# Weaving the second layer's mixer, in two token halves, into the expert retrieval of a two-layer decoder on one Trainium2 core

## The chip, the cores and the metric

The program runs on one core of one Trainium2 chip. All data are float32. The metric is the device time of one execution in microseconds (us). The time before is the median of three executions.

## The reference

Two decoder layers work on 512 tokens of width 1024. Each layer adds a mixer and then a channel mixer (PEER, a retrieval of experts) to the residual stream x; a last RMSNorm follows.

```
x = x + even_mixer(rmsnorm(x))          # layer 0: gated MLP and sparse attention
x = x + peer_0(rmsnorm(x))
x = x + odd_mixer(rmsnorm(x))           # layer 1: gated linear recurrence, 8 heads
x = x + peer_1(rmsnorm(x))
out = rmsnorm(x)

# peer: per token, 8 heads, the best 16 of 128 x 128 experts
s = (x @ w_q) . sub_keys                # two scores of 128 keys for each head
experts, gate = top16(sums of the two top16), softmax
u = u_tab[experts]; v = v_tab[experts]  # rows of 1024 + 1024 numbers
x += sum(gate * gelu(x . u) * v)

# odd_mixer, for each head: q, f, i, g = h @ w_in
fg = lb + (1 - lb) * sigmoid(f);  k = 1 - fg
state = diag(fg) state + k i^T;   o = q . state      # along the tokens, causal
out = (rmsnorm(o) * silu(g)) @ w_out
```

The recurrence of a token needs only tokens before it. The retrieval of a token needs only that token.

## The kernel before, in words

Every engine's program is written out by hand in full, in order, and the engines meet only by semaphores. There are four stages, one after the other: the even mixer, the retrieval of layer 0, the odd mixer, the retrieval of layer 1.

**Retrieval.** The 512 tokens are four blocks of 128. A block has 8 heads with 16 experts each, so there are 128 slots in a block and 512 in a layer. In a slot one expert row of 8 KB (u and v) is fetched for each of the 128 tokens, 1.05 MB, by an indirect DMA that POOL issues (L471) into one of 8 buffers of `gath` (region_g). VectorE forms the dot product of u and the normed token (L954, out in place). ScalarE's `weigh` takes the gelu (L619), multiplies by the gate (L620) and writes a diagonal matrix (L622). TensorE's `pair` multiplies this by v in two matmuls of 512 columns and adds up a whole block in PSUM banks 0 and 1 (L1338). POOL issues the gather of slot s + 8 once TensorE has done slot s. Between the dot products VectorE does the ranking (top 16, lookups) of the next head, and TensorE its query matmuls (L1293) and scores (L1308); the scores are copied from PSUM by VectorE (L876). ScalarE's softmax exponential (L613) needs another activation table than gelu, which is loaded again after it (the ACT_TABLE_LOAD rows).

**Odd mixer.** It starts when the last block of layer 0 has been added to x, with `normed_transposed(1)`. Per head, TensorE projects all 512 tokens (`projections`, L1388, L1391), builds the causal 128 x 128 products at 7 levels of a binary tree of distances and a diagonal (L1428), transposes and forms the state terms (L1435 to L1458). VectorE computes the running sum (L1054), the distances (L1067, L1068), the decayed queries (L1090) and puts each level into `attn` under a mask (L1072). ScalarE takes sigmoid (L678), logarithm (L688) and exponentials (L691), three activation tables. POOL multiplies the keys (L505). The weights come in slabs of 2 MB, one per head, into region_g, where the gather buffers also lie. Then the output projection, and the retrieval of layer 1 begins with its first routing and with the gathers after the last output projection.

Every engine waits for `primed` at the start; SyncE sets it after it has raised each event's semaphore by its starting value, so that waits for negative counts pass.

## Time and profile before

| | |
|---|---|
| median of three executions | 3622.25 us (3618.0 to 3626.44) |
| the profiled execution | 3623.28 us, span 3621.6 us |
| TensorE busy | 3090.3 us, 85% |
| VectorE busy | 2328.7 us, 64% |
| ScalarE busy | 1363.4 us, 38% |
| POOL busy | 1179.0 us, 33% |
| gathers (software queue) | 1073.81 MB, 71.5% of 16 engines' span |
| other transfers | 63.63 MB, 4.5% |
| mean granted TensorE clock | 0.939 |

Busy time is the sum of an engine's instructions; a group's mean is that of one instruction, and a float32 matmul is two of them (two MATMUL and two LDWEIGHTS records). What an instruction waited for stands behind it as the releaser of the idle time. The span has four stretches, which the windows of the trace show by their DMA share: up to 525 us, the first retrieval up to 1823 us, the odd mixer up to 2308 us, and the second retrieval.

### The profile page before, as it was taken

The page shows a single profiled execution, that of the slowest core. Times are in us where ns is not written, and L with a number is a line of the kernel's source. Part 1 is how long each engine was busy: PE and PEld are TensorE (multiplying, and loading weights), DVE is VectorE, ACT ScalarE, POOL GpSimd, SP SyncE. Part 2 cuts the span into 40 slices and gives each one's busy share as a digit, 9 for nine tenths or more (in the row PEclk, how much of TensorE's full clock was granted, in tenths as well). Part 3 has the DMA queues.
Part 4 walks back from the last instruction along what each step waited for, and adds up shares of the span by engine and source line. Part 5 has one row for each costly group of instructions (what it writes and reads, how often), then busy time and mean ns, then how long its engine had stood idle before and what let it go on. Part 6 is the DMA issues. An engine that isn't in the chain of part 4 may idle for free.

```text
span 3621.6 us, 31355 instructions
## 1 busy us (share of the span) xinstructions
PE 3090.3 (85%) x8800; PEld 1559.5 (43%) x8800; DVE 2328.7 (64%) x5547; ACT 1363.4 (38%) x3865; POOL 1179.0 (33%) x1164
## 2 busy tenths in 40 slices
PE   6988889888888888888878887888888888888887
PEld 3656644333333333333346665433333333333333
DVE  1144437777777777777745554577777777777777
ACT  0022204444444444444412222244444444444443
POOL 2000014444444434444401111243444444334443
PEclk9865589999999999999989998999999999999999
DMA  4120019999999999999941101499999999999998
GB/s 159 59 105 1 0 76 421 421 421 413 421 421 421 397 421 421 401 422 421 421 203 47 47 24 59 204 421 421 421 407 421 421 400 422 421 421 401 421 422 336
DMA packets 155535, 1139.45 MB, mean 315 GB/s; under 512 B 17888, under 2 KB 18144, under 8 KB 22240
## 3 DMA queue, kind: packets, MB, share of 16 engines
q0 software_dynamic: 147456, 1073.81, 71.5%
q1 hardware_dynamic: 7904, 63.63, 4.5%
q8 instruction: 70, 1.15, 0.1%
q14 instruction: 105, 0.86, 0.1%
HBM read 1134.23 MB, written 2.10 MB: 314 GB/s over the span
## 4 chain that ended last, share of the span: by engine, by line
DMA 42%; PE 38%; DVE 8%; ACT 6%; issue 3%; POOL 2%; DVEq 0%; SPq 0%; POOLq 0%; ACTq 0%
DMA region_g<-in_uv_dram,experts 42%; PE ps L1338 13%; DVE region_g L954 4%; PE ps L1388 4%; PE ps L1273 3%; PE ps L1391 2%; PE ps L1259 2%; PE ps L1293 2%; PE ps L1162 2%; PE ps L1221 2%; PE ps L1149 2%; PE ps L1428 1%; POOL region_g L471 1%; ACT region_c L622 1%; PE ps L1249 1%
## 5 line engine op out<-in xcount | busy, mean ns | idle before, releaser
L1338 PE MATMUL ps<-region_g,region_c 128*128 128x512 f32 x4096 | 1982.8, 613 | 370.2 <-ACT region_c L622 322.3
L954 DVE CUSTOM_DVE_ANT_0 region_g<-region_g,region_h 128x1024 f32<-128x1024 f32 x1024 | 1254.9, 1226 | 621.6 <-DMA region_g<-in_uv_dram,experts 607.2
L471 POOL DMA_INDIRECT region_g<-in_uv_dram,experts x1024 | 1089.4, 1064 | 1561.5 <-PE ps L1338 1413.5
L1338 PEld LDWEIGHTS ps<-region_g,region_c 128*128 128x128 f32 x4096 | 728.5, 191 | 1395.2 <-ACT region_c L622 767.5
L619 ACT ACTIVATE region_c<-region_c 128x1 f32<-128x1 f32 x1024 | 207.0, 202 | 1284.7 <-DVE region_c L954 1281.3
L622 ACT ACTIVATE region_c<-ident_z,region_c 128x128 f32<-128x128 f32 x1024 | 411.0, 401 | 33.5
L620 ACT ACTIVATE region_c<-region_c,gate 128x1 f32<-128x1 f32 x1024 | 301.4, 294 | 33.3
L1293 PE MATMUL ps<-region_a,region_h 128*128 128x256 f32 x1088 | 277.3, 379 | 0.0
L1293 PEld LDWEIGHTS ps<-region_a,region_h 128*128 128x128 f32 x1088 | 206.7, 190 | 139.0 <-issue 124.4
L1388 PE MATMUL ps<-region_h,region_g 128*128 128x512 f32 x256 | 134.6, 668 | 23.2 <-DVEq L1052 21.9
L1391 PE MATMUL ps<-region_g,region_h 128*128 128x256 f32 x512 | 118.8, 379 | 0.0
L1273 PE MATMUL ps<-region_g 128*128 128x512 f32 x256 | 114.6, 608 | 1.6 <-ACT region_g L603 0.8
L409 POOL TENSOR_SCALAR rstd<-stat 128x1 f32<-128x1 f32 (+2 forms) x9 | 3.6, 406 | 334.7 <-DVEq L848 306.7
L505 POOL TENSOR_TENSOR region_c<-region_g,region_c 128x256 f32<-128x256 f32 x56 | 42.5, 758 | 201.2 <-ACT region_c L691 131.6
L409 POOL TENSOR_SCALAR rstd<-mean 128x4 f32<-128x4 f32 x12 | 4.5, 377 | 306.3 <-DVEq L1115 156.3
L1391 PEld LDWEIGHTS ps<-region_g,region_h 128*128 128x128 f32 x512 | 94.1, 190 | 14.5 <-issue 3.8
L619 ACT ACT_TABLE_LOAD x66 | 84.7, 1283 | 14.6 <-DVE region_c L954 13.4
L1259 PEld LDWEIGHTS ps<-region_c 128*128 128x128 f32 x320 | 70.6, 328 | 38.0 <-issue 25.8
L1072 DVE COPY_PREDICATED region_c<-level_mask,ps 128x512 f32<-128x512 int32 x64 | 46.9, 733 | 59.1 <-PE ps L1428 58.7
L1388 PEld LDWEIGHTS ps<-region_h,region_g 128*128 128x128 f32 x256 | 51.9, 217 | 76.3 <-issue 74.6
L1259 PE MATMUL ps<-region_c 128*128 128x64 f32 x320 | 76.6, 426 | 8.9 <-ACT region_c L598 8.9
L954 DVE DVE_READ_ACCUMULATOR2_ANT region_c<- 128x1 f32 x1024 | 84.1, 82 | 0.0
(211 smaller groups left out, 2475.1 us busy)
## 6 DMA issues: line engine op xcount, KB each, us to landing
region_g<-in_uv_dram,experts POOLq DMA_INDIRECT x1024
region_g<-in_w_odd_dram SPq DMA_DIRECT2D x8, 2048.0 KB, 8.0
region_a<-in_w_even_dram SPq DMA_DIRECT2D x1, 5216.0 KB, 20.4
region_a<-in_w_even_dram SPq DMA_DIRECT2D x1, 4096.0 KB, 15.5
region_g<-in_w_out_e_dram SPq DMA_DIRECT2D x1, 4096.0 KB, 13.8
region_g<-in_w_out_o_dram SPq DMA_DIRECT2D x1, 4096.0 KB, 12.4
x_res<-in_x_dram SPq DMA_DIRECT2D x4, 512.0 KB, 5.0
region_a<-in_keys_dram SPq DMA_DIRECT2D x2, 1024.0 KB, 29.3
```

The lines of the kernel that those rows point to most:

```text
L471: g.indirect_dma_start(out=gath[:, k % NBUF, :], out_offset=None, in_=tab, in_offset=bass.IndirectOffsetOnAxis(ap=experts[:, e * TOPK + k: ...
L619: link(a.activation(gact[:, q:q + 1], dots[:, q:q + 1], ACT.Gelu_apprx_tanh))
L620: link(a.activation(wts[:, q:q + 1], gact[:, q:q + 1], ACT.Copy, scale=gate[:, e, k:k + 1]))
L622: a.activation(diag[:, k % NBUF, :], ident, ACT.Copy, scale=wts[:, q:q + 1]).then_inc(diag_ready.sem, 1)
L954: v.tensor_tensor_reduce(out=gath[:, buf, 0:D_MODEL], in0=gath[:, buf, 0:D_MODEL], in1=XNb[b % 2], scale=1.0, scalar=0.0, op0=ALU.mult, op ...
L1149: i = t.matmul(PS[:, 6 + ch % 2, :], We[:, c, TM_ALL + ch * P:TM_ALL + (ch + 1) * P], hT[:, c, :], start=c == 0, stop=c == KC - 1)
L1259: t.matmul(PS[:, 6 + par, br * HD:(br + 1) * HD], pTs[:, par, br * SEQ + kt * P:br * SEQ + (kt + 1) * P], vsw[:, kt, br, e * HD:(e + 1) * ...
L1273: i = t.matmul(PS[:, OUT_BANKS[tb] + j, :], mixT[:, c, tb * P:(tb + 1) * P], w[:, c, j * 512:(j + 1) * 512], start=c == 0, stop=c == KC - 1)
L1293: i = t.matmul(PS[:, 4, 0:256], hTb[:, c, :], wq[:, c, ds(hcol * 256, 256)], start=c == 0, stop=c == KC - 1)
L1338: i = t.matmul(PS[:, j, :], diag[:, k % NBUF, :], gath[:, k % NBUF, D_MODEL + j * 512:D_MODEL + (j + 1) * 512], start=first and e == 0 and ...
L1388: last = t.matmul(PS[:, j, :], W[:, c, j * P:(j + 1) * P], hT[:, c, :], start=c == 0, stop=c == KC - 1)
L1391: last = t.matmul(PS[:, 2 + tb // 2, (tb % 2) * 256:(tb % 2 + 1) * 256], hT[:, c, tb * P:(tb + 1) * P], W[:, c, 256:512], start=c == 0, st ...
```

## The change

- The order of the work is now one loop over 1024 slots, `for s in range(SLOTS)`, on each of VectorE, ScalarE, TensorE and POOL. The retrievals of both layers follow each other without a break. All other work of the second layer is cut into pieces, each with a slot number; a generator yields them, and `run(pieces, s)` emits those that are due after slot s.
- Layer 1's mixer works on halves of 256 tokens (two blocks). Half 0 is computed in slots 256 to 511, beside the retrieval of layer 0's blocks 2 and 3, half 1 in slots 512 to 767, beside layer 1's blocks 0 and 1. The state of each head is carried over in `carry`. Heads start 20 slots into such a stretch and every 19 slots.
- Routing (queries and scores) is done for two blocks at once, in four jobs, with transposed queries straight from the matmul; ScalarE copies the scores into a ring, VectorE no longer does.
- The weights come as 1 MB slabs into three buffers in region_a: 1 for each routing head, 2 for each recurrent head, 4 for the output projection. Each half and each pair of blocks fetches its weights again.
- In the two mixed stretches, slots 5 and 13 of each 16 are not multiplied by TensorE: VectorE adds gate * v to x (`row_added`, two slots later).
- Some of the recurrence's work moves from VectorE to ScalarE (the forget gate's affine step, the key decay, squares); all seven levels get their exponential in one instruction of 1792 columns.
- The starting values of the semaphores and `primed` are gone; waits for negative counts are left out of the program.

```diff
+HALF = 2 * P
+BLOCK = P_HEADS * TOPK
+PHASE = 2 * BLOCK
+SLOTS = DEPTH * TB * BLOCK
+HEADS_AT, HEAD_PACE = 20, 19
+DVE_ROWS = ((), (5, 13), (5, 13), ())
...
-            for e in events:
-                sp.sem_inc(e.sem, e.prime)
-            sp.sem_inc(primed, 1)
...
+            for q in range(2):
+                for h in range(C_HEADS):
+                    for part in range(2):
+                        slab(head_slab(q, h, part), w_odd[h][:, part * 2048:(part + 1) * 2048])
+                for j in range(4):
+                    slab(out_slab(q, j), w_out_o[:, 2 * j:2 * j + 2, :].rearrange("p c n -> p (c n)"))
+                for h in range(P_HEADS):
+                    routing_slab(2 + q, h)
...
+            def slab(i, dram):
+
+                if i >= 3:
+                    after(sp, *slab_user[i - 3])
+                sp.dma_start(slabs[i % 3][:, 0:KC * 256], dram).then_inc(slab_in[i % 3], 16)
...
+                    yield t0 + 1
+                    act.wait_ge(qf_done.sem, qf_done.at(n))
+                    act.wait_ge(ig_done.sem, ig_done.at(n))
...
+                    a.activation(kk, fgr, ACT.Identity, scale=-1.0, bias=ones[:]).then_inc(sig_ready.sem, 1)
+                    yield t0 + 2
+                    act.wait_ge(fg_ready.sem, fg_ready.at(n))
+                    a.activation(bb, fgr, ACT.Ln).then_inc(lf_ready.sem, 1)
...
+                    yield t0 + 6
+                    act.wait_ge(dd_ready.sem, dd_ready.at(n))
+                    a.activation(D, D, ACT.Exp)
+                    a.activation(eb, bb, ACT.Exp)
+                    for t in range(2):
+                        i = a.activation(kd[:, t * P:(t + 1) * P], bb[:, t * P:(t + 1) * P], ACT.Exp, scale=-1.0,
+                                         bias=bb[:, (t + 1) * P - 1:(t + 1) * P])
+                    i.then_inc(e_ready.sem, 1)
...
+                    yield t0 + 3
+                    dve.wait_ge(lf_ready.sem, lf_ready.at(n))
+                    link(v.tensor_tensor_scan(bb, scan_keep, bb, 0.0, ALU.mult, ALU.add))
...
+                    yield t0 + 7
+                    dve.wait_ge(e_ready.sem, e_ready.at(n))
...
+            def row_added(s):
+
+                n, k = s // TOPK, s % TOPK
+                c, xb = (n % 2) * TOPK + k, X[:, n // P_HEADS % TB, :]
+                dve.wait_ge(w_ready.sem, w_ready.at(dve_n(s)))
+                after(dve, vd_done, dve_n(s) - 1)
+                v.scalar_tensor_tensor(xb, gath[:, s % NBUF, D_MODEL:ROW], wts[:, c:c + 1], xb, ALU.mult, ALU.add
+                                       ).then_inc(vd_done.sem, 1)
...
+            for s in range(SLOTS):
+                n, k = s // TOPK, s % TOPK
+                dot_product(s)
+                if s >= 2 and on_dve(s - 2):
+                    row_added(s - 2)
+                if s % BLOCK == 2 and s > BLOCK:
+                    block_out(s // BLOCK - 1)
+                if k < 7:
+                    late_ranking(n + 1, k)
+                if k >= 12:
+                    early_ranking(n + 2, k - 12)
+                run(pieces, s)
...
+                        if h + 1 < C_HEADS and d < 19:
+                            projections(q, h + 1, d - 3)
...
+            for s in range(SLOTS):
+                if not on_dve(s):
+                    row_product(s)
+                run(pieces, s)
```

TensorE, in the middle of a head of the odd mixer, before: L1391 is a projection, L1428 a level, L1435 the key transposes, L1441 the state terms.

```order
L1428 MATMUL ps<-region_c 128x128 x4
L1391 MATMUL ps<-region_g,region_h 128x256 x4
L1428 MATMUL ps<-region_g 128x128 x4
L1391 MATMUL ps<-region_g,region_h 128x256 x4
L1435 MATMUL ps<-ident_z,region_c 128x128 x4
L1391 MATMUL ps<-region_g,region_h 128x256 x5
L1441 MATMUL ps<-region_g,region_c 128x128 x4
```

The same place in the change: L1566 is the row product of a slot, L1434 and L1437 are projections of the next head, L1475 two levels of a half, L1512 the key transposes.

```order
L1566 MATMUL ps<-region_g,x_res 128x512 x2
L1434 MATMUL ps<-region_a 128x256 x2
L1475 MATMUL ps<-region_a 128x128 x4
L1566 MATMUL ps<-region_g,x_res 128x512 x2
L1434 MATMUL ps<-region_a 128x256 x2
L1475 MATMUL ps<-region_a 128x128 x4
L1512 MATMUL ps<-ident_z,region_a 128x128 x2
L1437 MATMUL ps<-region_a 128x256 x2
L1566 MATMUL ps<-region_g,x_res 128x512 x2
```

Where projections and levels followed each other, a row product now stands before each group; one slot (between L1512 and the next L1437) has none, since VectorE takes its row.

ScalarE, at the start of a head in the change, after the last squares of the head before: L773, L774 and L780 are a slot's gelu, gate and diagonal, L724 to L729 the sigmoids, copies and the affine steps, L732 the logarithm.

```order
L724 ACT_TABLE_LOAD
L724 ACTIVATE region_a<-ps 128x256
L725 ACTIVATE region_a<-ps 128x256
L726 ACTIVATE region_a<-ps 128x256
L727 ACTIVATE region_a<-ps 128x256
L728 ACTIVATE region_a<-region_a,lb 128x256
L729 ACTIVATE region_a<-region_a,ones 128x256
L773 ACT_TABLE_LOAD
L773 ACTIVATE region_a<-region_a 128x1
L774 ACTIVATE region_a<-region_a,gate 128x1
L732 ACT_TABLE_LOAD
L732 ACTIVATE region_a<-region_a 128x256
```

Before, a sigmoid, a logarithm and the exponentials each loaded their table once in a head; now the gelu of the next slot needs its own table after each of them.

VectorE, at the same place in the change: L1153 is a slot's dot product with its accumulator, L989 to L993 the three operations that wait for the sigmoids, L996 the running sum that waits for the logarithm, L954 and L955 the distances.

```order
L989 TENSOR_SCALAR region_a<-region_a 128x256
L991 TENSOR_TENSOR region_a<-ps,region_a 128x256
L993 TENSOR_TENSOR region_a<-ps,region_a 128x256
L1153 ISA region_g,region_a<-region_g,region_h 128x1024
L1153 ISA region_a 128x1
L996 SCALAR_TENSOR_TENSOR region_a<-alibi,region_a 128x256
L1153 ISA region_g,region_a<-region_g,region_h 128x1024
L1153 ISA region_a 128x1
L954 TENSOR_TENSOR region_a<-region_a 128x128
L955 TENSOR_TENSOR region_a<-region_a 128x128
```

Between two operations that wait for ScalarE stands one dot product (and at most places a step of the ranking).

## Rows read from the trace of the kernel before

**Rows 1.** Windows: us, busy of each engine (xcount), granted clock, DMA share, GB/s.
```profile
525.00:1823.00 1298.00, 1110.26 (x2801) 495.34 (x2801) 955.41 (x2332) 577.72 (x1736) 545.56 (x514) 0.99 1.00 414
1823.00:2308.00 485.00, 408.47 (x1720) 278.34 (x1719) 238.57 (x450) 114.51 (x170) 54.13 (x77) 0.91 0.17 67
2308.00:3606.00 1298.00, 1110.16 (x2798) 494.46 (x2797) 958.24 (x2333) 577.69 (x1736) 548.71 (x516) 0.99 1.00 414
```
**Rows 2.** Timeline, POOL, the first gather of each retrieval and the last of the first: start, us.
```profile
525.31 1.23 POOL L471 DMA_INDIRECT region_g<-in_uv_dram,experts  x1 [44.29 <-PE ps L1273]
...
1807.10 0.94 POOL L471 DMA_INDIRECT region_g<-in_uv_dram,experts  x1 [0.31 <-issue]
...
2307.90 1.05 POOL L471 DMA_INDIRECT region_g<-in_uv_dram,experts  x1 [44.26 <-PE ps L1273]
```
**Rows 3.** Timeline, VectorE, the last dot product of the first retrieval and the first of the second.
```profile
1823.14 1.23 DVE L954 CUSTOM_DVE_ANT_0 region_g<-region_g,region_h 128x1024 f32<-128x1024 f32 x1 [1.21 <-DMA region_g<-in_uv_dram,experts]
...
2317.82 1.22 DVE L954 CUSTOM_DVE_ANT_0 region_g<-region_g,region_h 128x1024 f32<-128x1024 f32 x1 [0.18 <-DVE region_c L890]
```
**Rows 4.** Groups, 700 to 1700 us, shapes apart: group xcount | busy, mean ns | idle before, releasers.
```profile
L1338 PE MATMUL ps<-region_g,region_c 128*128 128x512 f32 x1585 | 766.4, 612 | 140.2 <-ACT region_c L622 116.9 <-DVEq L1000 17.1 <-issue 3.1
L954 DVE CUSTOM_DVE_ANT_0 region_g<-region_g,region_h 128x1024 f32<-128x1024 f32 x396 | 485.4, 1226 | 243.9 <-DMA region_g<-in_uv_dram,experts 239.1 <-DVE gstat L902 0.9 <-DVE gate L923 0.7
...
L622 ACT ACTIVATE region_c<-ident_z,region_c 128x128 f32<-128x128 f32 x396 | 158.9, 401 | 13.0
L620 ACT ACTIVATE region_c<-region_c,gate 128x1 f32<-128x1 f32 x396 | 116.6, 294 | 12.9
...
L619 ACT ACTIVATE region_c<-region_c 128x1 f32<-128x1 f32 x397 | 80.3, 202 | 501.3 <-DVE region_c L954 499.9
...
L619 ACT ACT_TABLE_LOAD x25 | 32.1, 1283 | 0.4
...
L876 DVE COPY region_c<-ps 128x256 f32<-128x256 f32 x25 | 10.5, 419 | 0.0
...
L627 ACT ACTIVATE region_c<-ps 128x256 f32<-128x256 f32 x25 | 9.2, 367 | 11.0 <-PE ps L1293 11.0
...
L860 DVE SCALAR_TENSOR_TENSOR region_h<-x_res,rstd,region_h 128x1024 f32<-128x1024 f32 x3 | 3.8, 1279 | 0.0
```
**Rows 5.** Timeline, TensorE: one row product alone and three in sequence.
```profile
1798.70 1.98 PE L1338 MATMUL ps<-region_g,region_c 128*128 128x512 f32 x4 [0.95 <-ACT region_c L622]
...
1801.38 5.31 PE L1338 MATMUL ps<-region_g,region_c 128*128 128x512 f32 x12
```
**Rows 6.** Groups, 1860 to 2260 us, the second layer's mixer, shapes apart.
```profile
L1391 PE MATMUL ps<-region_g,region_h 128*128 128x256 f32 x512 | 118.8, 379 | 0.0
...
L1428 PE MATMUL ps<-region_c 128*128 128x128 f32 x448 | 62.6, 286 | 12.3 <-DVE region_c L1090 11.8 <-issue 0.4
...
L1072 DVE COPY_PREDICATED region_c<-level_mask,ps 128x512 f32<-128x512 int32 x64 | 46.9, 733 | 59.1 <-PE ps L1428 58.7
...
L505 POOL TENSOR_TENSOR region_c<-region_g,region_c 128x256 f32<-128x256 f32 x56 | 42.5, 758 | 201.2 <-ACT region_c L691 131.6 <-PE ps L1428 69.6
L691 ACT ACTIVATE region_c<-region_c 128x512 f32<-128x512 f32 x56 | 35.3, 630 | 111.0 <-DVE region_c L1068 111.0
L1068 DVE TENSOR_TENSOR region_c<-region_g 128x256 f32<-128x256 f32 x56 | 28.1, 501 | 1.9
L1067 DVE TENSOR_TENSOR region_c<-region_g 128x256 f32<-128x256 f32 x56 | 24.2, 433 | 8.7 <-POOL region_c L505 6.4 <-DVE region_c L1072 0.9
...
L1054 DVE TENSOR_TENSOR_SCAN region_g<-alibi,region_g 128x512 f32<-128x512 f32 x8 | 9.8, 1224 | 1.6 <-ACT region_g L688 0.5
...
L1051 DVE TENSOR_TENSOR region_g<-ps,region_c 128x512 f32<-128x512 f32 x8 | 5.5, 692 | 1.2
```
**Rows 7.** Timeline, VectorE's first instruction.
```profile
6.61 0.06 DVE L718 MEMSET slope<- 128x1 f32 x1 [6.61 <-SPq L340]
```
**Rows 8.** The page's DMA issues: xcount, KB each, median us to landing.
```profile
region_g<-in_w_odd_dram SPq DMA_DIRECT2D x8, 2048.0 KB, 8.0
```

More of the change, by code:

```diff
@@ new lines, in dve_n, with row_freed, run, started @@
+        def dve_n(s):
+            return dve_rows[s + 1] - 1
+        def row_freed(eng, s):
+            if s < 0:
+                return
+            if on_dve(s):
+                after(eng, vd_done, dve_n(s))
+            else:
+                after(eng, slot_done, pe_n(s))
+        def run(pieces, tick):
+            while pieces[1] is not None and pieces[1] <= tick:
+                pieces[1] = next(pieces[0], None)
+        def started(gen):
+            return [gen, next(gen, None)]
@@ new lines, in final_norm @@
+                                       ).then_inc(fin_done.sem, 1)
+            link.reset()
+            pieces = started(mixer_pieces())
+            residual(0)
+            residual(1)
+            run(pieces, -90)
+            residual(2)
+            for step in range(4):
+                early_ranking(0, step)
+            for step in range(7):
+                late_ranking(0, step)
+            residual(3)
+            for step in range(4):
+                early_ranking(1, step)
+            run(pieces, -1)
@@ new lines, in mixer_pieces, with row_product @@
+            def mixer_pieces():
+                yield from routing_pieces(0)
+                yield from routing_pieces(1)
+                for q in range(2):
+                    yield from recurrence_pieces(q)
+                    yield from routing_pieces(2 + q)
+            def row_product(s):
+                b = s // BLOCK
+                first = all(on_dve(r) for r in range(b * BLOCK, s))
+                last = all(on_dve(r) for r in range(s + 1, (b + 1) * BLOCK))
+                if first:
+                    if b:
+                        after(pe, acc_out, b - 1)
+                    else:
+                        pe.wait_ge(wo_out.sem, wo_out.at(3))
+                pe.wait_ge(diag_ready.sem, diag_ready.at(pe_n(s)))
+                for j in range(2):
+                    i = t.matmul(PS[:, j, :], diag[:, pe_n(s) % NBUF, :],
+                                 gath[:, s % NBUF, D_MODEL + j * 512:D_MODEL + (j + 1) * 512], start=first, stop=last)
+                i.then_inc(slot_done.sem, 1)
```

1380 lines of the change are left out of this document (702 added, 678 removed).

## The prediction

> **What bounds the kernel now.** I read the windows first [rows 1]. Of the span, two stretches of 1298 us are retrieval, with the DMA engines busy all the time at 414 GB/s, and between them lie 485 us, the odd mixer, with a DMA share of 0.17. The timeline gives the edges [rows 2, 3]: the last dot product of layer 0 starts at 1823.14 us, the first gather of layer 1 at 2307.90 us. So for **484.8 us no gather moves**, although the gathers decide everything else. In a retrieval the groups say the same [rows 4]: VectorE's idle time before its dot products ends with a gather's landing (239.1 of 243.9 us), so a slot costs 1298 / 512 = 2.535 us, which is the DMA's time. The engines beside it have room: per slot VectorE is busy 955.4 / 512 = 1.866 us, TensorE 2.17 us, ScalarE 1.13 us, POOL 1.07 us [rows 1]. The change wants to put the mixer into that room.
>
> How deep is the buffer? The last gather was issued at 1807.10 and used at 1823.14 us [rows 2, 3], so 16.0 us, some 6 of the 8 slots, lie in the DMA queues. A stall of an engine of less than some 10 us costs nothing, as long as its mean load is under the DMA's. What counts is the mean over a head, 19 slots.
>
> **The sum**, against the profiled execution (3623.28 us, its span 3621.6 us; the median of the runs, 3622.25 us, is 1 us less).
>
> 1. The gap goes: **-484.8 us**. The restart goes too: the second retrieval's first dot product comes at 2317.82, 9.9 us after its first gather [rows 2, 3], against 2.5 us in the stream: **-7.4 us**.
>
> 2. Weights that now pass in the gather stream. In MB: a routing head's slab is 1.05 of queries and 0.13 of keys, 1.18. Job 0 leaves five of its eight to the stream (5.9), job 1 eight (9.4), jobs 2 and 3 sixteen (18.9), the two output projections 8.4: 42.6 MB outside the heads. Where the DMA binds, each MB costs 1 / 0.414 = 2.42 us: **+103 us**. There the other engines keep up: a routing head takes TensorE 16 matmuls of 256 columns at 0.464 us (below) and four of 128, some 8.5 us, with 6.1 row products of 1.77 us (below) 19.3 us in 7 slots, against (7 x 1.05 + 1.18) / 0.414 = 20.6 us of DMA. The heads' own slabs, 16 x 2.1 MB, are in the next term.
>
> 3. A recurrent head, 19 slots. **DMA:** (19 x 1.05 + 2.1) / 0.414 = 53.2 us.
>  **TensorE:** row products, 14 of 16, are 16.6. Three in sequence took 5.31 us, 1.77 us each, one alone 1.98 us [rows 5]; the group's mean is 766.4 / 396 = 1.94 us [rows 4]. I take 1.77, as a loaded TensorE has no waits between them: 29.4 us. 32 projection matmuls of 256 columns at 118.8 / 256 = 0.464 us: 14.8 us. 16 level matmuls of 128 columns at 62.6 / 224 = 0.28 us and ten other small ones at the same price: 7.3 us [rows 6]. Sum 51.5 us, with 1.94 us 54.3 us. It is under the DMA or equal to it.
>  **VectorE:** 19 x 1.866 = 35.5 us, less the score copy (0.42 us in each 16 slots, [rows 4]) 35.0 us. Its own small gaps: 2.535 - 1.866 - 239.1 / 396 = 0.065 us for a slot, 1.2 us. The rows it adds, 19 x 2 / 16 = 2.4, at the price of the 1024-column operation with two tensor inputs, 1.28 us [rows 4]: 3.0 us. The recurrence [rows 6]: an operation of 512 columns takes 0.692 us, one of 256 0.433 us, so one of 128 some 0.30 us. 14 distances and 7 decayed queries at 0.30 are 6.3 us; four products of 256 columns 1.7; eight masked copies, 0.733 us at 512 columns and so 0.45 at 256, 3.6; the running sum, 1.22 us at 512, 0.7; the floor of the gate 0.3; the state two of 128, 0.6; two outputs of 128, 0.6. Together 13.8 us. That is **53.0 us** of work, just what the DMA needs.
>  **The waits inside it.** VectorE waits for ScalarE three times in a head, and each time only one dot product and a step of ranking (1.8 us) lie between. A gelu, gate and diagonal take 0.20 + 0.29 + 0.40 us and a table load 1.28 us [rows 4]; activations of 256 and 512 columns take 0.37 and 0.63 us [rows 4, 6], so one of 1792 some 1.95 us. Sigmoids: 1.28 + six activations 2.3 = 3.6 us against 1.8: 1.8 us of wait. Logarithm: 1.28 for gelu, 0.9, 1.28, 0.4 = 3.9 us against 3.0 (one dot product and three operations): 0.9 us. Exponentials: 1.28 + 1.95 + 0.4 + 0.5 = 4.1 us against 1.8: 2.3 us. Sum 5.0 us. In about one head of five a softmax with its two table loads falls into one of these: 0.5 us. No row shows this interplay, so I bound it: nothing if the DMA is late anyway, 10 us if each wait doubles.
>  **POOL against VectorE:** seven key products in each head, while VectorE works. The two halves of a distance are alike in size, and take 0.501 and 0.433 us on average [rows 6]; put down to POOL altogether, as an upper reading of this row, that is 0.07 us for each product, 0.5 us a head.
>  So VectorE needs 53.0 + 5.0 + 0.5 + 0.5 = **59.0 us** for 19 slots that took 19 x 2.535 = 48.2 us. **+10.8 us for each of 16 heads, +173 us.** With the DMA alone it would be +5.1, with full contention and doubled waits +18.
>
> 4. Edges: before the first head of a half TensorE has 16 projection parts in 8 slots, 3.4 us a slot against 2.5, and ScalarE waits for the last; the output projection's parts weigh 1.7 us a slot. I take 4 us for each half, **+8 us** (0 to 20).
>
> 5. The start. All engines waited until 6.61 us for SyncE's semaphores [rows 7]: -6.1 us. Ahead of the first gather TensorE now routes two blocks instead of one, with a second set of transposes and its copy, +5 us. Together **-1 us**.
>
> 3623.3 - 484.8 - 7.4 + 103 + 173 + 8 - 1 = **3414 us**.
>
> The tail (last slot to stored rows) keeps its steps. POOL has 20.2 us of gathers in a head and adds 7 products of some 0.4 us: covered, since it is idle until TensorE frees a slot. ScalarE has 21.4 us of slots and some 16 us of its own (six table loads, 7.7, and activations) in 59: covered on average.
>
> **Two rules of the Trainium skill.** Behind the 0.07 us: the page SBUF — State Buffer, section Who interferes with whom, has VectorE and GpSimd lock each other out for a whole instruction when VectorE reads two SBUF tensors and GpSimd reads SBUF. By it each key product (0.758 us at 256 columns, an estimated 0.43 at 128) would hold VectorE up for its full length, 3.0 us a head instead of 0.5, and the sum would be 3454 us; the row of the distances shows much less. Behind the routing slabs, whose rows are 1 KB long: the page DMA: Bandwidth & Descriptors, section Why small descriptors are slow, gives three extra cycles for each packet, 35 for 32 at 1 KB; no run here shows it, and the sum would be an estimated 8 us more.
>
> **Rivals.**
> - **The DMA binds throughout.** If ScalarE runs ahead of my count, all 76.2 MB of slabs cost 184 us and the mixer nothing more: 3623.3 - 484.8 - 7.4 - 1 + 184 = 3314 us. For it: the 16 us queue. Against it: VectorE's 53.0 us leave no room for any wait.
> - **The engines wait for each other.** TensorE's six middle slots of a head carry levels as well: 6 x 1.77 + 6 x 0.93 + 5.5 = 21.7 us, against 18.6 us at 3.1 us a slot. VectorE waits for these levels two slots later, and then TensorE for VectorE's rows. With 64 us a head it is 80 us more, 3494 us. For it: 54.3 us of TensorE at the price of single rows. Against it: the two slots of distance are 6 us.
> - **Slower: the slabs come late.** The second slab of a head is asked for when the head before has been projected, and TensorE wants it 6 slots (18.6 us) later. The gathers of [rows 2, 3] took 16.0 us through the full queue; a slab that has to queue behind gathers and another slab would stall TensorE in the middle of its rows. TensorE's 51.5 us plus the stall pass 59 us from 7.5 us on. To lose the whole gain, a head would need 59.0 + 209 / 16 = 72.1 us, so a stall of 21 us, a slab landing after 39 us. At 45 us it is 78.5 us a head, 312 us more: 3726 us. For it: nothing in this trace shows both queues loaded. Against it: 2 MB with no gathers beside them took 8.0 us [rows 8], and at half the rate 16.
> - **The stream breaks.** If the routing of layer 1's first blocks is not ready at slot 512, gathers stop after all. It ends only 8 slots before. The price would be some 60 us of the 485 saved, inside my range.
>
> **Chances.** My case 60%. DMA throughout 15%. Mutual waits 20%. Slabs late enough to be slower 4%, about no change 1%. The range of 8 in 10 reaches from 3325 (between my case and the first rival) to 3530 (the second rival with doubled waits). A measurement of this kernel tells 0.2%, 7 us. Faster by more: 0.95, within: 0.01, slower: 0.04.
>
> **What would show it.** Right: no stretch without gathers between 525 us and the end; windows inside the heads at some 373 GB/s (22.0 MB in 59 us), with VectorE busy over 0.9 and its waits on ScalarE's sigmoid, logarithm and exponential (1.8, 0.9, 2.3 us); outside them 414 GB/s. Wrong: heads at 414 GB/s (first rival), TensorE busy all the time or VectorE waiting for L1475 (second), TensorE waiting for a landing from in_w_odd (third).

## The result and the profile after

The changed kernel takes 3436.09 us (median, 3431.08 to 3439.38) against 3622.61 us for the kernel before in the same series: ratio 0.9484, 95% interval 0.9466 to 0.9503. Forecast were 3414 us, range 3325 to 3530. The profiled execution took 3432.9 us, its span is 3430.4 us.

The windows of the changed kernel; they answer to [rows 1]: the first stretch of retrieval without heads, the heads of half 0, the routing behind them, the heads of half 1, and the last stretch. Columns: us, busy of PE, PEld, DVE, ACT, POOL, granted clock, DMA share, GB/s.

```profile
543.00:1232.00 689.00, 588.73 (x1596) 285.63 (x1596) 447.36 (x1141) 297.25 (x867) 275.10 (x259) 0.99 1.02 415
1283.00:1755.00 472.00, 408.75 (x1390) 240.64 (x1389) 381.34 (x995) 268.09 (x652) 212.72 (x222) 0.95 0.95 374
1793.00:2004.00 211.00, 184.50 (x589) 106.05 (x590) 137.06 (x330) 85.38 (x246) 84.80 (x77) 0.98 1.02 413
2055.00:2530.00 475.00, 413.94 (x1398) 244.77 (x1398) 378.30 (x987) 267.52 (x652) 215.11 (x222) 0.94 0.94 371
2770.00:3417.00 647.00, 512.59 (x1022) 183.43 (x1022) 438.30 (x1084) 278.08 (x831) 267.61 (x257) 0.97 1.00 414
```

The stretch at 67 GB/s is gone. There are two kinds of stretch now: 414 GB/s outside the heads, some 372 inside. The timeline of POOL with the first gather, which answers to [rows 2], and that of VectorE with the first and the last dot product, to [rows 3]:

```profile
531.40 1.25 POOL L568 DMA_INDIRECT region_g<-in_uv_dram,experts  x1 [29.30 <-PE ps L1362]
```

```profile
543.60 1.23 DVE L1153 CUSTOM_DVE_ANT_0 region_g<-region_g,region_h 128x1024 f32<-128x1024 f32 x1 [0.18 <-DVE region_c L1081]
...
3416.70 1.23 DVE L1153 CUSTOM_DVE_ANT_0 region_g<-region_g,region_h 128x1024 f32<-128x1024 f32 x1 [1.22 <-DMA region_g<-in_uv_dram,experts]
```

Since every slot has one dot product, their starts cut the span exactly. Before, a slot of the stream was 2.5206 us from dot product to dot product. Now the 719 slots outside the heads take 1926.5 us, 114.1 more than at that price; the 304 slots of the heads take 471.5 + 475.1 = 946.6 us, 180.4 more; the first dot product comes 8.4 us later than before (535.2 us); the tail is 1.9 us shorter. With the 492.2 us of the gap: 3621.6 - 492.2 + 114.1 + 180.4 + 8.4 - 1.9 = 3430.4 us, the measured span.

What VectorE waits for in the heads of half 0 (1283 to 1755 us): us in total, times, longest.

```profile
DVE region_a L969 <- PE ps L1475: 23.1, 17, 4.6
DVE region_a L1040 <- POOL ost L521: 19.6, 6, 5.7
DVE region_a L961 <- ACT region_a L741: 13.9, 8, 3.0
DVE region_a L996 <- ACT region_a L732: 7.5, 8, 1.4
DVE region_a L989 <- ACT region_a L729: 7.4, 3, 6.1
```

And TensorE, in the same stretch:

```profile
PE ps L1566 <- ACT x_res L780: 58.5, 30, 6.3
```

Per head VectorE is busy 381.34 / 8 = 47.7 us and waits 11.3; TensorE is busy 408.75 / 8 = 51.1 us and waits 7.9, nearly all for a slot's diagonal (L780). Neither is busy throughout. The waits for the levels (L1475) and for POOL's root of the output (L521) are not in the forecast's account of a head.

TensorE's granted clock falls in the heads too, to 0.95 and 0.94 from 0.99 in the first stretch. In half 0, 44 of the 471.5 us lie at the lower of its two levels (1.2 GHz instead of 2.4), in nine short stretches; each begins during a wait of TensorE of 2.6 to 6.3 us or at most 1.1 us behind it. So TensorE pays for some of its waits a second time.

### The profile page after: what moved, and what is told of

Read it like the earlier page. It is cut to its first block, busy times and chain, and to the rows that moved or that the text cites. A ratio compares the mean times of both kernels' runs of the same rounds, so it can differ in the third digit from the quotient of the medians.

```text
span 3430.4 us, 30594 instructions
## 1 busy us (share of the span) xinstructions
PE 2927.8 (85%) x8568; PEld 1548.4 (45%) x8568; DVE 2226.7 (65%) x5636; ACT 1459.7 (43%) x3950; POOL 1258.2 (37%) x1254
## 4 chain that ended last, share of the span: by engine, by line
PE 43%; DMA 31%; DVE 12%; ACT 10%; issue 3%; POOL 2%; DVEq 0%; SPq 0%; POOLq 0%; ACTq 0%
DMA region_g<-in_uv_dram,experts 29%; PE ps L1566 19%; DVE region_g L1153 6%; PE ps L1400 3%; PE ps L1437 3%; PE ps L1348 2%; PE ps L1251 2%; PE ps L1310 2%; PE ps L1362 2%; PE ps L1238 2%; PE ps L1434 2%; DMA region_a<-in_keys_dram 1%; ACT x_res L780 1%; POOL region_g L568 1%; PE ps L1475 1%
## 5 line engine op out<-in xcount | busy, mean ns | idle before, releaser
L1566 PE MATMUL ps<-region_g,x_res 128*128 128x512 f32 x3840 | 1896.2, 624 | 414.6 <-ACT x_res L780 379.3
L1153 DVE CUSTOM_DVE_ANT_0 region_g<-region_g,region_h 128x1024 f32<-128x1024 f32 x1024 | 1255.4, 1229 | 572.6 <-DMA region_g<-in_uv_dram,experts 561.2
L1566 PEld LDWEIGHTS ps<-region_g,x_res 128*128 128x128 f32 x3840 | 705.1, 196 | 1350.3 <-ACT x_res L780 733.6
L773 ACT ACTIVATE region_a<-region_a 128x1 f32<-128x1 f32 x1024 | 208.7, 204 | 1372.9 <-DVE region_a L1153 1367.5
L780 ACT ACTIVATE x_res<-ident_z,region_a 128x128 f32<-128x128 f32 x960 | 387.4, 404 | 31.2
L774 ACT ACTIVATE region_a<-region_a,gate 128x1 f32<-128x1 f32 x1024 | 304.5, 297 | 33.4
L1400 PE MATMUL ps<-region_a 128*128 128x256 f32 x1024 | 243.8, 383 | 5.5 <-DMA region_a<-in_keys_dram 4.3
L1400 PEld LDWEIGHTS ps<-region_a 128*128 128x128 f32 x1024 | 196.5, 192 | 83.5 <-issue 55.4
L773 ACT ACT_TABLE_LOAD x110 | 141.1, 1283 | 6.4 <-DVE region_a L1153 4.4
L1434 PE MATMUL ps<-region_a 128*128 128x256 f32 x512 | 133.7, 391 | 0.0
L1437 PE MATMUL ps<-region_a 128*128 128x256 f32 x512 | 131.2, 383 | 0.0
L1434 PEld LDWEIGHTS ps<-region_a 128*128 128x128 f32 x512 | 101.4, 199 | 63.3 <-issue 54.7
L1437 PEld LDWEIGHTS ps<-region_a 128*128 128x128 f32 x512 | 97.7, 192 | 59.3 <-issue 51.8
L969 DVE COPY_PREDICATED region_a<-level_mask,ps 128x256 f32<-128x256 int32 x128 | 56.7, 443 | 61.7 <-PE ps L1475 52.5
L1153 DVE DVE_READ_ACCUMULATOR2_ANT region_a<- 128x1 f32 x1024 | 84.6, 83 | 0.0
L1162 DVE SCALAR_TENSOR_TENSOR x_res<-region_g,region_a,x_res 128x1024 f32<-128x1024 f32 x64 | 82.0, 1281 | 0.0
L765 ACT ACT_TABLE_LOAD x63 | 80.8, 1283 | 1.1
```

The lines of the kernel that those rows point to most:

```text
L765: a.activation(gexp, best, ACT.Exp, bias=gstat[:, 0:1], accum_out=gstat[:, 1:2]).then_inc(gexp_out.sem, 1)
L773: link(a.activation(gact[:, c:c + 1], dots[:, c:c + 1], ACT.Gelu_apprx_tanh))
L774: i = a.activation(wts[:, c:c + 1], gact[:, c:c + 1], ACT.Copy, scale=gate[:, n % 2, k:k + 1])
L780: a.activation(diag[:, pe_n(s) % NBUF, :], ident, ACT.Copy, scale=wts[:, c:c + 1]).then_inc(diag_ready.sem, 1)
L1153: v.tensor_tensor_reduce(out=u_, in0=u_, in1=XNr[n // P_HEADS % 3], scale=1.0, scalar=0.0, op0=ALU.mult, op1=ALU.add, accum_out=dots[:, c: ...
L1162: v.scalar_tensor_tensor(xb, gath[:, s % NBUF, D_MODEL:ROW], wts[:, c:c + 1], xb, ALU.mult, ALU.add).then_inc(vd_done.sem, 1)
```

## Experiments

Each kernel ran in one series with the kernel before; ratios are to it (its median lies between 3622.6 and 3625.2 us in the five series). "Less" and "slower" in us are against the 3436.09 us of the changed kernel. Runs 3, 4 and 11 are single executions. "Heads" are the 152 slots of half 0 and of half 1, by the dot products (160 in runs 10 and 12). A head's tick d is the d-th slot after its start; a piece of tick d stands behind that slot's work.

**1. POOL's root earlier.** The head's root is placed ahead of one more gather in POOL's program.

```diff
-                        yield head_tick(q, h) + 19
+                        yield head_tick(q, h) + 18
                         pool.wait_ge(oss_ready.sem, oss_ready.at(n))
```

> POOL does the small root for a head's output right after it has issued the gather of slot t0 + 26 instead of t0 + 27, so before it waits for slot t0 + 19 to come free. Theory (in the heads VectorE is the bound, and its waits add up): its wait for this root, 25.6 us in the eight heads of the first half (3.2 us a head), mostly goes; 2 to 3 us a head, 16 heads, less what shows up in another wait: the changed kernel's 3436 us become 3395 to 3415 us, the heads 56 to 57 us instead of 58.9 us. Rival 1 (the DMA engines bind in the heads): no change, heads 58.9 us. Rival 2 (TensorE and VectorE hold each other up at the levels): the wait moves to the levels, less than 10 us gained.

Measured: 3435.17 us, ratio 0.9474 (0.9459 to 0.9490): no difference to 0.9484 that can be told. VectorE's waits in the heads of half 0:

```profile
DVE region_a L969 <- PE ps L1475: 30.4, 18, 5.8
DVE region_a L989 <- ACT region_a L729: 15.4, 8, 6.2
...
DVE region_a L996 <- ACT region_a L732: 10.5, 8, 1.9
DVE region_a L1040 <- POOL ost L521: 10.5, 5, 3.6
```

The root's wait is half as long, and what it gave was taken by the next wait in program order, the sigmoids of the next head (7.4 before), and by the levels. The heads take 478.4 and 475.3 us; run 8, which changes nothing in them, also has 478.4 and 474.6, so some 7 us of half 0 are scatter. In run 8 it goes with TensorE's clock. Its window of half 0:

```profile
1281.00:1760.00 479.00, 416.58 (x1391) 244.65 (x1390) 382.32 (x995) 267.06 (x652) 210.63 (x222) 0.93 0.94 369
```

The same program of a head, with 65 instead of 44 us at the lower level, keeps TensorE busy 7.8 us more and takes 6.9 us more. VectorE's busy time is the same within 1 us. Not all of the scatter is the clock: run 7, also unchanged in the heads, has 474.3 us at 0.95.

**2. VectorE adds no rows.** `DVE_ROWS` is empty in all stretches.

> No row is added by VectorE; TensorE multiplies all 16 of 16 in the mixed stretches too. Theory (VectorE bounds the heads): it loses 2.4 x 1.28 = 3.0 us of work a head and POOL no longer waits for rows that VectorE frees late; TensorE gets 4.2 us more, 51.5 + 4.2 = 55.7 us, which is under 58.9 us. So the heads get 1 to 3 us shorter, and the whole 15 to 45 us faster than the changed kernel, if nothing else binds. Rival 2 (TensorE and VectorE hold each other up at the levels): TensorE at 55.7 us plus its wait is the bound, heads 60 us or more, the whole 15 us or more slower. Outside the heads, routing beside 16 of 16 rows: TensorE 7 x 1.77 + 8.5 = 20.9 us in 7 slots against 20.6 us of DMA, no change or a few us slower.

Measured: 3450.31 us, ratio 0.9515 (0.9499 to 0.9531), 14 us slower. The heads take 484.8 and 482.9 us. The window of the heads of half 0 and VectorE's largest waits in it:

```profile
1285.00:1770.00 485.00, 437.90 (x1470) 254.47 (x1469) 359.26 (x976) 274.16 (x671) 208.72 (x222) 0.96 0.95 365
```

```profile
DVE region_a L969 <- PE ps L1475: 37.6, 24, 4.6
DVE region_a L1040 <- POOL ost L521: 34.4, 6, 8.6
```

VectorE's busy time falls from 381.3 to 359.3 us, TensorE's rises from 408.8 to 437.9 us. So a head is not VectorE's work plus fixed waits: 2.8 us less of that work a head made it 1.7 and 1.0 us longer in the two halves, and VectorE's waits for the levels and for POOL's root, which stands behind slots that TensorE frees, grew. This is the side of the expectation's rival. The rows on VectorE are worth their place.

**3, 4. Fewer bytes.** In 3 each slab of a head after the first three brings an eighth of its bytes (`dram[:, 0:256]`), in 4 each routing slab of the queries after the first three does (`k_ = 1` of 8 chunks). The matmuls run on what lies in the buffers: seven eighths of those weights are left out.

> Left out: of each recurrent head's slab after the first three only 1 of 8 KB in each partition is loaded, so these projections use old weights and the output is another. 29 slabs shrink by 0.92 MB, 27 MB in all. Theory (VectorE and its waits bound the heads): the heads stay at 58 to 59 us, the whole is within 10 us of the changed kernel's profiled execution (3433 us). Rival 1 (the DMA binds in the heads): 27 x 2.42 = 65 us faster.

> Left out: of each routing head's query weights after the first three slabs only one of eight chunks is loaded, so the scores are others and other experts are fetched, as many as before. 29 slabs shrink by 0.92 MB, 26.6 MB in all. Theory (outside the heads the DMA binds, and every MB costs 2.42 us): 64 us faster than the changed kernel, about 3369 us; phase 0 takes 689 - 29 = 660 us. If rows of 1 KB cost more than their bytes, more than that: 70 to 90 us. Rival (TensorE binds while it routes beside the rows in the two mixed stretches): less than 45 us.

Measured: 3424.92 us and 3366.18 us. The window of the heads of half 0 in 3, and that of the first 256 slots in 4:

```profile
1283.00:1754.00 471.00, 408.01 (x1388) 240.59 (x1387) 381.18 (x995) 266.16 (x653) 212.14 (x222) 0.95 0.91 349
```

```profile
543.00:1202.00 659.00, 584.44 (x1594) 289.08 (x1595) 448.32 (x1148) 295.22 (x864) 289.60 (x258) 0.98 1.01 417
```

With 7% fewer GB/s the heads take the same 471 and 475 us: there the DMA does not bind. Outside, 4 moves its fewer bytes at 417 GB/s, as before (415), and 689 us become 659. By the dot products the stretches outside the heads take 69.4 us less, where the bytes alone say 64: there the DMA binds by bytes.

**5. Projections early.** The 16 projection parts of the next head stand two to a slot at the head's ticks 3 to 8, and at 15 to 18, instead of one to a slot from 3 to 18.

```diff
+PARTS_AT = {3: (0, 1), 4: (2, 3), 5: (4, 5), 6: (6, 7), 7: (8, 9), 8: (10, 11), 15: (12,), 16: (13,), 17: (14,), 18: (15,)}
...
-                        if h + 1 < C_HEADS and d < 19:
-                            projections(q, h + 1, d - 3)
+                        if h + 1 < C_HEADS:
+                            for part in PARTS_AT.get(d, ()):
+                                projections(q, h + 1, part)
```

> The projections of the next head move from the ticks 3 to 18 (one each) to the ticks 3 to 8 (two each) and 15 to 18. Theory (a head is a first part in which VectorE waits for ScalarE and TensorE waits with it, and a second part in which TensorE carries rows, projections and levels and VectorE waits for it): the wait of VectorE for the levels, 3.4 us a head, and part of the wait of TensorE for ScalarE, 58.5 us in eight heads, go away, a head falls from 59.0 to 54 to 55 us, the kernel by 60 to 70 us, to about 3370 us. Rival (VectorE's own work and its waits for ScalarE set a head alone): the wait only moves, as it did when POOL's root came earlier, and the time stays at 3436 +- 5 us. Second rival (the second slab of a head is asked for late): TensorE waits for the slab of in_w_odd at tick 4, and the time rises.

Measured: 3399.92 us, ratio 0.9384 (0.9369 to 0.9400), 36 us less. The heads take 455.5 and 455.6 us. VectorE's and TensorE's waits (half 0):

```profile
DVE region_a L1041 <- POOL ost L522: 16.6, 6, 3.9
DVE region_a L970 <- PE ps L1476: 15.2, 9, 4.2
```

```profile
PE ps L1568 <- ACT x_res L781: 45.3, 26, 6.8
```

The direction is the theory's, the size 55% of it. The same TensorE work in another order gives 16 and 19.5 us a half: the forecast's account of a head, which had TensorE hidden at 51.5 us, can't give that. It was not the first part of the head that gained. TensorE's waits before the slots of ticks 7 to 10 fall from 20.5 to 2.3 us in half 0; those at ticks 2 to 4 stay (35.7 and 36.6 us).

**6. Key products on VectorE.** The seven products of a head move from POOL to VectorE, behind the decayed queries of the same levels.

> The seven key products of a head move from POOL to VectorE. Theory (VectorE is held up while POOL reads SBUF for them): the decayed queries fall from a mean of 0.468 to 0.29 us, some 2.7 us of contention a head go, VectorE's added work is 7 x 0.20 = 1.4 us, so a head falls by 1.3 us and the kernel by 20 us, more if the levels come earlier too. Rival (the longer decayed queries are only waits for ScalarE's exponential in other dress, no contention): VectorE gets 1.4 to 3 us a head more and the kernel is 20 to 50 us slower.

Measured: 3423.82 us, ratio 0.9447 (0.9431 to 0.9463), 12 us less; heads 469.0 and 469.6 us. First what happens in the changed kernel, POOL and VectorE at the same time (start, us, ..., count):

```profile
1314.32 3.09 POOL L547 TENSOR_TENSOR region_a<-region_a 128x128 f32<-128x128 f32 x7
```

```profile
1311.44 0.90 DVE L961 TENSOR_TENSOR region_a<-region_a 128x128 f32<-128x128 f32 x4 [2.99 <-ACT region_a L741]
...
1314.44 3.32 DVE L961 TENSOR_TENSOR region_a<-region_a 128x128 f32<-128x128 f32 x3
```

Four products alone take 0.90 us, three under POOL's seven 3.32 us, and both engines end within 0.4 us of each other. The groups of the decayed queries in the changed kernel, then in this one (L954), with the key products (L960):

```profile
L961 DVE TENSOR_TENSOR region_a<-region_a 128x128 f32<-128x128 f32 x56 | 23.0, 468 | 14.0 <-ACT region_a L741 13.9
```

```profile
L954 DVE TENSOR_TENSOR region_a<-region_a 128x128 f32<-128x128 f32 x56 | 12.8, 286 | 13.9 <-ACT region_a L734 13.8
L960 DVE TENSOR_TENSOR region_a<-region_a 128x128 f32<-128x128 f32 x56 | 12.6, 281 | 0.0
```

The contention is real: (23.0 - 12.8) / 8 = 1.3 us a head here, with the two products behind it (0.526 and 0.524 us each, now 0.414) some 1.5. My 2.7 was one head's worst. The Trainium skill's rule (SBUF — State Buffer, Who interferes with whom: an operation of VectorE with two inputs in SBUF and one of GpSimd that reads SBUF exclude each other) agrees with the 3.32 us. VectorE's added work is 1.6 us, about as much, and its busy time falls by only 4.0 and 3.3 us a half. So the contention does not account for the 12 us; what else gives them is not shown, and the two halves' 2.5 and 5.5 us are within their scatter.

**7. Routing weights by head.** The host lays `w_q` out so that a slab is one row of 8 KB in each partition instead of eight of 1 KB.

```diff
-        "w_q": arr("peer_w_q").reshape(2, 8, 128, 2048).transpose(0, 2, 1, 3),
+        "w_q": arr("peer_w_q").reshape(2, 8, 128, 8, 256).transpose(0, 2, 3, 1, 4).reshape(2, 128, 8, 2048),
```

> The routing weights are laid out head by head, so that a slab is one row of 8 KB per partition instead of eight of 1 KB. Bytes and the rest stay. Where the DMA binds, outside the heads, 40 slabs of 1.05 MB pass in 1 KB packets. By bytes alone: no change. By the three extra cycles of the Trainium skill's page DMA: Bandwidth & Descriptors (35 for 32): 8 us less. By the packets' mean times (47 to 49 ns for these, 39 ns for those of linear slabs): up to 19 us less. All of it has to show in the stretches outside the heads, phase 0 and the routing after the heads; the heads stay at 471 and 475 us.

Measured: 3418.31 us, ratio 0.9432 (0.9417 to 0.9448), 18 us less than the changed kernel's. By the dot products the three stretches with routing slabs fall from 688.7, 248.8 and 240.3 to 682.7, 243.7 and 236.1 us, together 15.3 us; the heads stay within 3 us. The queue of the slabs on the two pages (packets, MB, share), the changed kernel's and this one's:

```profile
q1 hardware_dynamic: 50576, 102.96, 8.0%
```

```profile
q1 hardware_dynamic: 21904, 102.96, 7.5%
```

The same bytes in 28672 fewer packets. They belong to 32 slabs (the expectation says 40), of which three are loaded ahead of the stream, so 25984 packets go in these stretches: 15.3 us of 16 engines are 9.4 ns for each. The packets' own mean times agree: 48.8 ns for one of 1 KB, 315.9 for one of 8 KB, 39.5 for each KB. The Trainium skill's page DMA: Bandwidth & Descriptors, section Why small descriptors are slow (three extra cycles a packet, 35 for 32 at 1 KB), gave an estimated 8 us; the sign agrees, the size measured here is twice that. Run 4 took the same number of packets away with their bytes and gained only 5 us beyond the bytes; why not 15 is open.

**8. The start's order.** In job 0 ScalarE takes the second block's squares before it copies the first block's transposed rows.

> At the start ScalarE takes the squares of the second block before it copies the transposed rows of the first. Theory (TensorE is idle for 4.44 us before the transposes of the second block because of this order): the first gather comes 4 to 5 us earlier, at 527 us instead of 531.4, and the kernel is 4 to 5 us faster. Rival (the first gather waits for the slabs or for TensorE's queue): no change.

Measured: 3432.30 us (3427.24 to 3437.85), ratio 0.9469 (0.9453 to 0.9485), not to be told from 0.9484 by itself. In the trace the first gather starts at 527.10 us instead of 531.40 and the first dot product at 539.3 instead of 543.6: 4.3 us, as expected.

**9. Four together** (5, 6, 7, 8).

> The four edits together: projections early, key products on VectorE, routing weights by head, the start's order. If their gains add, 35.6 + 11.7 + 17.2 + 3.2 = 67.7 us below the changed kernel's 3436, 3368 us. The gains outside the heads (routing weights 17, start 3) have nothing in common with the others and must stay. In the heads the projections and the key products may gain less together (both free VectorE or what it waits for): 3368 to 3380. Or more, if TensorE, now with levels on time, lets VectorE use the contention's time in full: 3355 to 3368.

Measured: 3381.67 us, ratio 0.9327 (0.9312 to 0.9343). The gains don't add (54 of 68 us): the heads take 461.1 and 456.0 us, no less than with 5 alone, so the key products on VectorE are worth nothing that can be told once the levels come in time. Outside the heads 7 and 8 kept theirs.

**10. The same at 20 slots a head.** `HEADS_AT, HEAD_PACE = 20, 20`.

> As e9, and a head takes 20 slots instead of 19, so that eight slots of each half move from the routing's stretch into the heads. Theory (in the heads the engines bind, outside the DMA by its bytes): a slot less outside is 1.05 MB less at 414 GB/s, 2.54 us; a slot more in the heads costs what VectorE has to do for it, 1.87 us, or less where it falls into a wait: 16 slots give 11 us or more, up to 20, so 3348 to 3357 us against 3368 for e9. Rival (in the heads the DMA binds by bytes as well, or latencies grow with the slots): no change against e9.

Measured: 3361.87 us, ratio 0.9276 (0.9261 to 0.9292), 20 us less than 9. TensorE's wait for the diagonals in the heads of half 0 and their window:

```profile
PE ps L1574 <- ACT x_res L776: 41.0, 33, 4.4
```

```profile
1271.00:1744.00 473.00, 426.22 (x1425) 246.64 (x1424) 393.25 (x1098) 276.36 (x679) 191.32 (x175) 0.95 0.98 393
```

The eight further slots cost 11.5 and 13.8 us in the heads and give 25.7 and 24.7 in the stretches behind them. Work is moved from where the DMA binds to where it has room.

**11. No tables in the mixer.** Copies of the same size in place of the mixer's sigmoids, logarithm and exponentials; those functions are left out.

> The changed kernel with ScalarE's sigmoids, logarithm and exponentials of the mixer replaced by copies of the same size, so that the four to six table loads of a head go (this leaves out those functions of the computation; the routing that follows is of other numbers, of the same shapes). Theory (in the first part of a head VectorE waits for ScalarE and TensorE with it): 3.6 us of VectorE's waits a head and most of the 58.5 us that TensorE waits for ScalarE in eight heads go, a head falls from 59.0 to 54 to 56 us, the kernel by 50 to 80 us, to 3355 to 3385 us. Rival (TensorE's overload in the second part sets a head by itself, and the ScalarE waits fill time that it leaves): the kernel falls by less than 20 us.

Measured: 3383.88 us, 52 us less; the heads take 449.6 and 450.0 us, 56.2 us a head. TensorE's wait:

```profile
PE ps L1566 <- ACT x_res L780: 39.7, 28, 3.6
```

Its fall, 58.5 - 39.7 = 18.8 us, is most of the 21.9 us that the heads of half 0 lose; in half 1 it is 14.5 of 25.1. In half 0 the waits before the slots of tick 2 fall from 23.4 to 4.3 us; it is there that ScalarE's table loads for the sigmoids and the logarithm stood. VectorE's three waits for ScalarE fell as well, from 28.8 to some 12 us, so this run alone does not say which engine's wait counts; run 12 speaks for TensorE's.

**12. The exponentials in two.** On 10: the first four levels' exponential signals by itself, and VectorE starts on them.

```diff
-                    a.activation(D, D, ACT.Exp)
+                    a.activation(D[:, 0:4, :], D[:, 0:4, :], ACT.Exp).then_inc(e_half.sem, 1)
+                    a.activation(D[:, 4:LEVELS, :], D[:, 4:LEVELS, :], ACT.Exp)
```

> As e10, and ScalarE's exponential of 1792 columns is two, of the first four levels (1024 columns) and of the other three; VectorE's first decayed queries wait for the first alone. It then goes on 1.8 us earlier (the rest of 1.70 us, 0.40 and two of 0.39 us come behind it), so its wait of 13.4 us in eight heads goes. Theory (VectorE's waits for ScalarE in the first part of a head lie on the path of the lockstep, since TensorE waits with it): 1.0 to 1.7 us a head, 16 to 27 us, 3335 to 3346 us. Rival (as with POOL's root in e1, a wait taken away in one place comes back at the next, the levels of TensorE or the root): within 5 us of e10's 3362.

Measured: 3360.59 us, ratio 0.9269 (0.9256 to 0.9282). The rival holds. VectorE's waits in 10 and in 12:

```profile
DVE region_a L971 <- PE ps L1482: 21.7, 10, 5.7
...
DVE region_a L957 <- ACT region_a L737: 13.4, 8, 3.0
```

```profile
DVE region_a L972 <- PE ps L1484: 30.1, 12, 6.9
...
DVE region_a L958 <- ACT region_a L734: 3.3, 4, 1.4
```

10.1 us of wait for ScalarE went, 8.4 came back as wait for TensorE's levels, and TensorE's own wait for diagonals stayed (41.0, 41.3).

**What sets a head.** By the slot that TensorE waits to multiply, its 58.5 us of waiting in the changed kernel lie at ticks 2 to 4 (36 us) and 7 to 10 (20 us); in 10 they are at ticks 2 to 4 (30 of 41 us), and after those TensorE is busy almost without a gap. That is how 5 gained (it put work into ticks 3 to 8, and the waits at 7 to 10 went) and why 12 did not (it shortened a wait of VectorE where TensorE had work anyway). How much of 5's gain is these waits filled and how much is ticks 9 to 14 left free for the levels, no run parts. The beginning of the sixth head of half 0 in the timeline of the changed kernel (start, us, the wait before it in brackets), POOL first, then ScalarE, VectorE, TensorE:

```profile
1583.71 1.95 POOL L568 DMA_INDIRECT region_g<-in_uv_dram,experts  x1 [2.22 <-PE ps L1566]
1586.29 0.93 POOL L568 DMA_INDIRECT region_g<-in_uv_dram,experts  x1 [0.63 <-PE ps L1566]
...
1587.60 0.72 POOL L521 TENSOR_TENSOR ost<-ost,half 128x2 f32<-128x2 f32 x1
```

```profile
1586.22 1.28 ACT L724 ACT_TABLE_LOAD   x1
...
1589.39 0.51 ACT L729 ACTIVATE region_a<-region_a,ones 128x256 f32<-128x256 f32 x1
1589.92 1.28 ACT L773 ACT_TABLE_LOAD   x1
...
1591.76 1.28 ACT L732 ACT_TABLE_LOAD   x1
...
1595.35 0.40 ACT L780 ACTIVATE x_res<-ident_z,region_a 128x128 f32<-128x128 f32 x1
```

```profile
1588.41 0.61 DVE L1040 SCALAR_TENSOR_TENSOR region_a<-ps,ost,region_a 128x128 f32<-128x128 f32 x2 [2.31 <-POOL ost L521]
1589.93 0.29 DVE L989 TENSOR_SCALAR region_a<-region_a 128x256 f32<-128x256 f32 x1 [0.91 <-ACT region_a L729]
```

```profile
1586.25 1.98 PE L1566 MATMUL ps<-region_g,x_res 128*128 128x512 f32 x4 [0.24 <-ACT x_res L780]
...
1595.81 2.08 PE L1566 MATMUL ps<-region_g,x_res 128*128 128x512 f32 x2 [6.30 <-ACT x_res L780]
```

ScalarE's squares for the root had ended at 1583.9, but in POOL's program two gathers stand ahead of it, and each needs a slot that TensorE frees. VectorE waits for that root and then for the sigmoids; no dot product starts from 1583.6 to 1590.8, so ScalarE, with four table loads of 1.28 us on its way, makes no diagonal between 1586.2 and 1595.35 us (the one slot in between is a row that VectorE adds), and TensorE has no row to multiply from 1588.2 to 1595.8 us. This is the longest such case; the mean over 30 is 2 us. It can't have worked ahead: at ticks 11 to 15 VectorE waits for the levels within two slots of TensorE, so no rows are in store.

## Why the prediction was right

The time came out 22 us above the forecast, well inside the range, and its large terms hold. Of the profiled execution's 19 us, the start is 9, the heads 7, the stretches outside them 3, less 2 for the tail. The step inside a head does not hold as it was reasoned: two errors of 4.6 us each cancelled, too much work and too few waits on VectorE. That its 59.0 us were met is luck.

The prediction's own signs are mixed. No stretch without gathers, 414 GB/s outside the heads and 374 and 371 inside came as forecast. VectorE busy over 0.9 did not (0.81 and 0.80), and the second rival's sign, VectorE waiting for L1475, did appear.

- **The gap, -492.2 us:** right. No break at slot 512 either; that rival did not occur.
- **Slabs outside the heads, +103 and edges +8:** measured 114.1. Run 4 shows the price per byte; run 7 shows that 15 us of it are the 1 KB packets, which the sum had left out beside the rule that named them. The edge before a half's first head did not appear: those 20 slots take 51.1 and 50.8 us, against 50.4 at the price of a slot. One working is off: in the first 256 slots TensorE multiplies all rows, so a routing head is 7 x 1.77 + 8.5 = 20.9 us there, not 19.3; the DMA bound all the same.
- **TensorE in a head, 51.5 us:** measured 51.1, but at a granted clock of 0.95, which the forecast does not have.
- **VectorE's work in a head, 53.0 us:** 1.2 us of it were small gaps; with the 0.5 us of contention the busy time was forecast at 52.3 us, and 47.7 were measured. The rows that it adds are as priced (24.3 us for 19 in eight heads, 3.0 us a head). By their rows in the trace, dot products and ranking cover 263.7 us in eight heads, 33.0 a head (35.0 forecast), the recurrence's operations (L954 to L1040) 105.2 us, 13.2 a head with the contention in them (14.3 forecast), and 1.6 us a head the two overlap each other. The recurrence was added up by mean lengths, but short operations overlap: one of 128 columns counts 0.286 us, the four above took 0.90. Without run 6's 1.5 us of contention that term, 13.8 us, was some 2 us too high.
- **VectorE's waits, 5.0 us:** with the small gaps and the softmax 6.7 us of idle time were forecast, 11.3 measured. For ScalarE they are 3.6 us (1.7, 0.9, 0.9 for exponential, logarithm, sigmoid; 2.3, 0.9, 1.8 forecast). Not foreseen were POOL's root, 3.2 us with what the trace puts down to issue, and the levels, 3.4 us with the same.
- **"It is under the DMA or equal to it":** this is the step that failed. A TensorE of 51.1 us in 59 looked hidden, and the head was priced by VectorE alone. Run 2 (less work on VectorE, more on TensorE, slower), run 5 (TensorE's order alone, 36 us) and run 8 (a lower clock in half 0, longer by as much as TensorE's busy time) show that TensorE's work and its place in the head count in full; runs 11 and 12 show that a wait for ScalarE counts where TensorE starves with it (22 and 25 us a half) and not where it has work (nothing). The rival "the engines wait for each other" had this mechanism and the wait for L1475; its size, 64 us a head, was too high, the measured 58.9 and 59.4 are those of my own case.
- **Contention with POOL, 0.5 us a head:** 1.5 us by run 6, between my reading of the old rows (0.5) and the Trainium skill's rule as I priced it (3.0).
- **The DMA binds throughout:** excluded by run 3. **Slabs late:** TensorE shows no wait for a slab in the heads; excluded in this kernel.
- **Start, -1 us:** +8.4. The engines do start at once (VectorE's first instruction at 0.87 us instead of 6.61), and TensorE's output projection began 6.6 us earlier; but from there to the first gather it is 76.9 us instead of 64.1. Routing two blocks costs 12.7 us, not 5; run 8 shows 4.3 of them to be an order on ScalarE, and TensorE's timeline has most of the rest as work: query matmuls of 8.86 us ahead of the first gather instead of 3.62, and 1.97 us of transposes of the second block. From the first gather to the first dot product it is another 2.3 us more (12.2 against 9.9).
- **A slab that lands after 45 us:** the prediction's working gives 51.5 + 26.4 = 77.9 us a head by its own numbers, not 78.5. Nothing hung on it.

Still open: whether root and sigmoids moved together would free ticks 1 to 3; run 1 moved only the root. It was not tried. Runs 10 and 12 are the fastest versions, 0.9276 and 0.9269, and can't be told apart; both beat the changed kernel by some 75 us and the kernel before by some 263.

## What to carry to other kernels

When work is woven into a stream, account for every engine by place, not only by its mean: an engine at 87% can be the bound if it starves in one part of the period and is overloaded in another, and then the order of its work is worth more than its amount. Price a wait by what the engine behind it does meanwhile; if that engine has work in store, taking the wait away gives little (here nothing that could be measured). Where two stretches have different limits, move work from the one that the DMA binds to the one that has DMA to spare.

## What the runs showed of the hardware

- Short independent VectorE operations overlap: a mean length of 0.286 us in run 6, but four in sequence in 0.90 us. A sum of means overstates a chain of them.
- Three VectorE products of 128 columns under seven of POOL's took 3.32 us instead of some 0.7 (three quarters of the 0.90), while POOL took 3.09 us for its seven.
- In run 7 each 1 KB packet that 8 KB rows save is worth some 9.4 ns of one DMA engine; the window of the first stretch rises from 415 to 419 GB/s. Run 4 gives less, some 3 ns.
- TensorE's granted clock went to the lower level (1.2 GHz) for some us in the heads, each time during or right behind a wait of 2.6 to 6.3 us: 44 of 471.5 us in half 0 of the changed kernel, 65 of 478.4 in run 8, whose heads are the same program and took 6.9 us more.
